# A two-layer decoder block on one core: the rotary key stored over 128 rows, the compressed query taken unnormalised from the accumulators, and the low part of the next key placed between mask and maximum

## The reference, cut to what matters

```python
def mla_mixer(h, w_dq, q_norm, w_uq, w_o, k_nope, k_rope, v, cos_rh, sin_rh):
    cq = rms_norm(h @ w_dq, q_norm)
    q = (cq @ w_uq).reshape(bsz, s_len, B_HEADS, QK_NOPE_DIM + QK_ROPE_DIM)
    q_nope = q[..., :QK_NOPE_DIM]                                  # 128 wide
    q_rope = apply_rope(q[..., QK_NOPE_DIM:], cos_rh, sin_rh)      # 64 wide
    ...
        logits = (einsum(qn, k_nope) + einsum(qr, k_rope)) * scale # 8 heads, k_rope shared by all
        logits = where(kpos <= qpos, logits, -inf)
        p = softmax(logits)
        return einsum(p, v)
```

## Time and profile before

| | |
|---|---|
| Median of three runs | 2006.02 us |
| Profiled execution, its own time | 2004.04 us |
| Its span, first to last instruction | 2001.7 us |
| PE busy | 1953.9 us (98%) |
| DVE, ACT, POOL busy | 967.7, 701.1 and 56.0 us |
| Mean granted TensorE clock | 0.991 of full |

### The profile page before, as it was taken

The page is one execution under the profiler, slowest core; times in us unless marked ns, Lnnn a source line. Parts: engine busy times, 40 slices in busy tenths (PEclk is TensorE's granted clock), DMA queues, the critical chain, the costliest instruction groups (busy, mean ns, idle before and its releaser), DMA issues.

```text
span 2001.7 us, 25843 instructions
## 1 busy us (share of the span) xinstructions
PE 1953.9 (98%) x9999; PEld 1662.5 (83%) x9999; DVE 967.7 (48%) x1399; ACT 701.1 (35%) x1095; POOL 56.0 (3%) x56
## 2 busy tenths in 40 slices
PE   7999999989999999999999999999899999999998
PEld 5888888978889888888998888889777898888888
DVE  5544432467655544442285444324766464444323
ACT  3332322345535323232253232223555442332222
POOL 0000000011100000000000000000000000000000
PEclk9999999999999999999999999999999999999999
DMA  5333333312213232333223333332211223333331
GB/s 159 102 88 105 87 95 109 88 43 84 74 54 95 84 105 84 105 87 108 80 76 104 105 90 99 95 97 83 58 38 53 64 64 105 100 89 102 98 95 43
DMA packets 344630, 174.64 MB, mean 87 GB/s; under 512 B 12159, under 2 KB 344045, under 8 KB 344557
## 3 DMA queue, kind: packets, MB, share of 16 engines
q1 hardware_dynamic: 341728, 171.47, 30.1%
q10 hardware_dynamic: 2828, 2.15, 0.4%
HBM read 171.50 MB, written 2.10 MB: 87 GB/s over the span
## 4 chain that ended last, share of the span: by engine, by line
PE 91%; DVE 5%; ACT 2%; issue 1%; DMA 1%; POOL 0%; SPq 0%; ACTq 0%; DVEq 0%
PE acc L1344 26%; PE acc L1346 26%; PE acc L1345 26%; PE sco L1344 3%; PE sco L1346 3%; PE sco L1345 3%; PE aux L1372 1%; DVE xT L941 1%; DVE y L934 1%; ACT prob_odd L656 1%; PE acc L1528 1%; DMA raw<-in_ffn_w_dram 1%; ACT tmp L644 1%; DVE mx L1061 1%; PE aux L1379 1%
## 5 line engine op out<-in xcount | busy, mean ns | idle before, releaser
L1344 PE MATMUL acc<-xg,wh 128*128 128x512 f32 (+1 forms) x1832 | 687.8, 375 | 15.4 <-DVE kh L1255 4.5
L1346 PE MATMUL acc<-xg,wl 128*128 128x512 f32 (+1 forms) x1832 | 680.5, 371 | 0.0
L1345 PE MATMUL acc<-xg,wh 128*128 128x512 f32 (+1 forms) x1832 | 680.3, 371 | 0.0
L876 DVE TENSOR_TENSOR wl<-raw,wh 128x1024 fp32r<-128x1024 f32 (+1 forms) x332 | 385.8, 1187 | 178.6 <-ACT wh L530 172.3
L1344 PEld LDWEIGHTS acc<-xg,wh 128*128 128x128 f32 x1832 | 346.3, 189 | 78.9 <-issue 4.4
L1345 PEld LDWEIGHTS acc<-xg,wh 128*128 128x128 f32 x1832 | 346.2, 189 | 60.0 <-issue 1.7
L1346 PEld LDWEIGHTS acc<-xg,wl 128*128 128x128 f32 x1832 | 346.1, 189 | 59.5
L530 ACT ACTIVATE wh<-raw 128x1024 fp32r<-128x1024 f32 (+1 forms) x332 | 327.0, 1023 | 141.6 <-PE acc L1346 86.0
L1346 PE MATMUL acc<-hT,wl 128*128 128x512 f32 (+1 forms) x704 | 255.2, 362 | 0.0
L1345 PE MATMUL acc<-hT,wh 128*128 128x512 f32 (+1 forms) x704 | 255.2, 362 | 0.0
L1344 PE MATMUL acc<-hT,wh 128*128 128x512 f32 (+1 forms) x704 | 255.2, 362 | 0.0
(11 more groups left out here) (221 smaller groups left out, 1847.5 us busy)
## 6 DMA issues: line engine op xcount, KB each, us to landing
raw<-in_ffn_w_dram SPq DMA_DIRECT2D x240, 512.0 KB, 4.3
raw<-in_ffn_w_dram SPq DMA_DIRECT2D x32, 384.0 KB, 3.5
raw<-in_moba_w_qkv_dram SPq DMA_DIRECT2D x24, 512.0 KB, 3.8
raw<-in_moba_w_o_dram SPq DMA_DIRECT2D x8, 512.0 KB, 3.8
raw<-in_mla_w_o_dram SPq DMA_DIRECT2D x8, 512.0 KB, 4.1
raw<-in_mla_w_dq_dram SPq DMA_DIRECT2D x4, 512.0 KB, 4.0
raw<-in_mla_w_uq_dram SPq DMA_DIRECT2D x8, 256.0 KB, 2.9
raw<-in_w_ukv_dram SPq DMA_DIRECT2D x16, 128.0 KB, 3.5
```

Of the source, the lines that this page charges most:

```text
L876: v.tensor_tensor(wl[:, slot, 0:tiles], raw[:, slot, 0:tiles], f32(wh[:, slot, 0:tiles]), ALU.subtract).then_inc(w_lo, 1)
L1344: t.matmul(dst, w_h, m_h, start=start, stop=False)
L1345: t.matmul(dst, w_h, m_l, start=False, stop=False)
L1346: return t.matmul(dst, w_l, m_h, start=False, stop=stop)
```

## The change: what it does

Three parts, all in the MLA stage:

- The rotary key `krT` is stored once for each half, with the other 64 rows zero (multiplied by a mask column `row_half`), so that the rotary products of `scores` run over all 128 rows. This is one more ACT copy and one more DVE operation at the entry.
- The compressed query is no longer normalised. ACT writes its high part `cqT` from each accumulator as soon as its unit is done, and squares it from there; DVE writes the low part from the accumulator. `spread(N_PRE4)`, the copy to `Rb`, the four multiplications and one POOL power go; the first normalisation enters through the variance (`xvar`) from which `qscale` is made. Here `split(4)`, `split(5)`, `split(6)` stand apart instead of in a row.
- `softmax_max` is cut in two, `softmax_mask` and `softmax_max`, and in MLA the low part of the next key stands between them.

The mask now lies on top of `ck`, so POOL writes it after the low parts of `ckT` and `krT`, and the buffers of values, outputs and odd probabilities get other places. In MoBA the two softmax functions are called one behind the other, in the order of before.

```diff
+        mask = at("mask", [P, P], F32, base[0])
...
+        neghalf = sb("neghalf", [P, TS + 2])
+        row_half = neghalf[:, TS:TS + 2]
...
+        xvar = rsums
...
-        krT = over("krT", [P, 2, S], F32R)
+        krT = over("krT", [P, 2, 2, S], F32R)
...
-        cq = at("cq", [P, KQ, S], F32, oT_at)
+        cqT = at("cqT", [P, 2, KQ, S], F32R, oT_at)
+
+        oM = (at("oM_hi", [P, HEADS, S], F32R, xg_base), at("oM_lo", [P, HEADS, S], F32R, oT_at + 4 * HEADS * S))
...
             if n == N_CQ:
-                return (cosR, sinR)[i % 2]
+                return (cosR, sinR, T[2])[i - 1]
...
         def values_of(n):
 
-            if n < HEADS:
-                return vh[:, n % 2, 0], vh[:, n % 2, 1]
-            return tuple(xg[:, a, KQ + n % 2].rearrange("p (t d) -> p t d", d=P) for a in range(2))
+            return vh[:, n % 2, 0], vh[:, n % 2, 1]
+
+        def o_of(n, a):
+
+            return oT[:, a, n] if n < HEADS else oM[a][:, n - HEADS]
+
+        def q_of(_):
+
+            return lambda k: (cqT[:, 0, k], cqT[:, 1, k])
...
             post_norm(N_F2)
-            causal_mask(3, U0[5])
-            rsqrt(EV0[N_PRE4])
+            pool.wait_ge(cq_lo, KK + 2)
+            causal_mask(3)
             rope_add(4 * HEADS + 8, T[3][:])
-            rsqrt(EV0[N_CQ])
...
             def square(n, i, src):
 
-                bufs = 1 if n in POST_FFN else 2 if n == N_CQ else 3
+                bufs = 1 if n in POST_FFN else 3
...
                 s.activation(ckT[:, 0, i], ck[:, i], COPY).then_inc(cq_hi, 1)
-            s.activation(krT[:, 0], ck[:, KK], COPY).then_inc(cq_hi, 1)
-            for w in (4, 5, 6):
-                split(u + w)
-            for m in range(KQ):
-                act.wait_ge(evacuated, r + m + 1)
-                if m == 0:
-                    act.wait_ge(unit_done, u + KQ)
-                s.activation(xg[:, 0, m], cq[:, m], COPY, scale=gains[:, G_Q + m:G_Q + m + 1]
+            for i in range(2):
+                s.activation(krT[:, i, 0], ck[:, KK], COPY, scale=row_half[:, i:i + 1]).then_inc(cq_hi, 1)
+
+            def cq_hi_of(m):
+                act.wait_ge(unit_done, u + m + 1)
+                s.activation(cqT[:, 0, m], acc[m][:], COPY, scale=gains[:, G_Q + m:G_Q + m + 1]
                              ).then_inc(cq_hi, 1)
+                square(N_CQ, m, acc[m][:])
+
+            split(u + 4)
+            cq_hi_of(0)
+            split(u + 5)
+            cq_hi_of(1)
+            cq_hi_of(2)
+            cq_hi_of(3)
+            split(u + 6)
...
             direct("k", 0, kh[:, 0])
             probT_zeros()
-            for m in range(KQ):
-                square(N_CQ, m, cq[:, m])
             v_split(HEADS)
...
-            def softmax_max(n):
+            def softmax_mask(n):
 
                 dve.wait_ge(score_psum, 3 * (n + 1))
                 if n % HEADS == 0:
...
+
+            def softmax_max(n):
+
                 for c in range(TS):
                     bank, o = BANK[c]
                     ins = v.tensor_reduce(mx[:, c:c + 1], sco[bank][:, o:o + (c + 1) * P], AX_X, ALU.max)
...
+            for i in range(2):
+                v.memset(row_half[i * ROPE:(i + 1) * ROPE, i:i + 1], 1.0)
+                v.memset(row_half[(1 - i) * ROPE:(2 - i) * ROPE, i:i + 1], 0.0)
...
             x_squares(N_PRE4)
-            norm_var(N_PRE4)
             for i in range(KK):
                 dve.wait_ge(cq_hi, i + 1)
                 v.tensor_tensor(ckT[:, 1, i], ck[:, i], f32(ckT[:, 0, i]), ALU.subtract).then_inc(cq_lo, 1)
-            dve.wait_ge(cq_hi, KK + 1)
-            v.tensor_tensor(krT[:, 1], ck[:, KK], f32(krT[:, 0]), ALU.subtract).then_inc(cq_lo, 1)
-            norm_diag(N_PRE4, 0, 1.0, T[3])
-            for w in (4, 5, 6):
-                split(u + w)
-            norm_factor(N_PRE4)
-            for m in range(KQ):
-                dve.wait_ge(unit_done, u + m + 1)
-                v.tensor_tensor(cq[:, m], acc[m][:], Rb[:], ALU.mult).then_inc(evacuated, 1)
-            dve.wait_ge(evacuated, r + KQ)
-            for m in range(KQ):
-                dve.wait_ge(cq_hi, KK + 1 + m + 1)
-                v.scalar_tensor_tensor(out=xg[:, 1, m], in0=cq[:, m], scalar=gains[:, G_Q + m:G_Q + m + 1],
-                                       in1=f32(xg[:, 0, m]), op0=ALU.mult, op1=ALU.subtract).then_inc(cq_lo, 1)
+            for i in range(2):
+                dve.wait_ge(cq_hi, KK + i + 1)
+                v.scalar_tensor_tensor(out=krT[:, i, 1], in0=ck[:, KK], scalar=row_half[:, i:i + 1],
+                                       in1=f32(krT[:, i, 0]), op0=ALU.mult, op1=ALU.subtract).then_inc(cq_lo, 1)
+
+            def cq_lo_of(m):
+                dve.wait_ge(cq_hi, KK + 2 + m + 1)
+                dve.wait_ge(sq_ready, SQ0[N_CQ] + m + 1)
+                v.scalar_tensor_tensor(out=cqT[:, 1, m], in0=acc[m][:], scalar=gains[:, G_Q + m:G_Q + m + 1],
+                                       in1=f32(cqT[:, 0, m]), op0=ALU.mult, op1=ALU.subtract
+                                       ).then_inc(evacuated, 1)
+
+            split(u + 4)
+            cq_lo_of(0)
+            dve.wait_ge(var_psum, EV0[N_PRE4] + 1)
+            v.tensor_scalar(xvar[:], aux[:, 0:TS], EPS, None, ALU.add).then_inc(r_ready, 1)
+            split(u + 5)
+            for m in range(1, KQ):
+                cq_lo_of(m)
+            split(u + 6)
...
             dve.wait_ge(var_psum, EV0[N_CQ] + 1)
-            v.tensor_scalar(var[:], norm_bank[0][:, 0:TS], EPS, None, ALU.add).then_inc(var_ready, 1)
-            dve.wait_ge(rtok_ready, EV0[N_CQ] + 1)
+            dve.wait_ge(r_ready, EV0[N_PRE4] + 1)
+            v.scalar_tensor_tensor(out=var[:], in0=xvar[:], scalar=EPS, in1=norm_bank[0][:, 0:TS],
+                                   op0=ALU.mult, op1=ALU.add).then_inc(var_ready, 1)
+            dve.wait_ge(rtok_ready, RT0[N_CQ] + 1)
             v.tensor_scalar(qscale[:], rtok[:], B_SCALE, None, ALU.mult).then_inc(r_ready, 1)
             dve.wait_ge(r_ready, EV0[N_CQ] + 1)
...
-                softmax_max(n)
+                softmax_mask(n)
                 if nxt:
                     direct("k", h + 1, kh)
+                softmax_max(n)
                 if turn:
                     rotated()
                 if nxt:
...
-                        if not first and (p, k) == (1, 6):
+                        if not first and (p, k) == (1, 6) and n_pre != N_PRE4:
                             spread(n_pre)
...
                     ins = product(dst, qh[:, 0, c * P:(c + 1) * P], qh[:, 1, c * P:(c + 1) * P],
-                                  kh[:, 0, 0:w], kh[:, 1, 0:w], True, rope_rows is None)
-                    if rope_rows is not None:
-                        rr = slice(rope_rows, rope_rows + ROPE)
-                        ins = product(dst, qrT[rr, 0, c * P:(c + 1) * P], qrT[rr, 1, c * P:(c + 1) * P],
-                                      krT[rr, 0, 0:w], krT[rr, 1, 0:w], False, True)
+                                  kh[:, 0, 0:w], kh[:, 1, 0:w], True, rope is None)
+                    if rope is not None:
+                        ins = product(dst, qrT[:, 0, c * P:(c + 1) * P], qrT[:, 1, c * P:(c + 1) * P],
+                                      krT[:, rope, 0, 0:w], krT[:, rope, 1, 0:w], False, True)
                     if c:
                         ins.then_inc(score_psum, 1)
```

More of the change, by code:

```diff
@@ L93, in yoco_kernel @@
     EV0 = [sum(2 if i in POST_FFN + POST_WO else 1 for i in range(n)) for n in range(15)]
-    SPREAD0 = [EV0[n] - (n > N_CQ) for n in range(14)]
+    RT0 = [EV0[n] - (n > N_PRE4) for n in range(14)]
+    SPREAD0 = [RT0[n] - (n > N_CQ) for n in range(14)]
     SQ_LAST0 = [2 * sum(LAST[:n]) for n in range(14)]
@@ L200, in yoco_kernel @@
         oT = over("oT", [P, 2, HEADS, S], F32R)
-        cq = at("cq", [P, KQ, S], F32, oT_at)
+        cqT = at("cqT", [P, 2, KQ, S], F32R, oT_at)
+        oM = (at("oM_hi", [P, HEADS, S], F32R, xg_base), at("oM_lo", [P, HEADS, S], F32R, oT_at + 4 * HEADS * S))
         assert spot[0] <= h_base + 4 * 2 * KF * S
-        prob_odd = [at(f"prob_odd{i}", [P, POFF[TS]], F32, o) for i, o in enumerate((ckT_at, vh_at))]
+        prob_odd = [at(f"prob_odd{i}", [P, POFF[TS]], F32, o)
+                    for i, o in enumerate((ckT_at, xg_base + 4 * KD * S))]
         BANK = [(0, 2 * P), (0, 0), (1, 0), (2, 0)]
@@ L487, in rope_add, with causal_mask @@
                 g.tensor_tensor(dst, T[0][:], T[2][:], ALU.add).then_inc(roped, 1)
-            def causal_mask(count, free_after):
-                pool.wait_ge(unit_done, free_after)
+            def causal_mask(count):
                 g.memset(mask[:], 0.0).then_inc(mask_ready, 1)
@@ L1500, in att_dst, with scores @@
                 return att_banks[st][rr][:]
-            def scores(n, rope_rows=None):
+            def scores(n, rope=None):
                 if n:
@@ L1558, in out_proj, with heads_out @@
                 last = heads + HEADS - 1
+                def heads_out(cols=slice(0, S)):
```

(17 more changed lines are left out.)

33 lines of the change are left out of this document (17 added, 16 removed).

## The result

The changed kernel takes 1995.23 us (median of 5 runs, 1994.26 to 1995.87), the kernel before, run beside it, 2004.49 us (5 runs). The two medians differ by 9.3 us. The ratio on record, 0.9945 with a 95% interval of 0.9934 to 0.9956, is not the quotient of the two medians (0.9954) and stands for 11 us, 9 to 13: the changed kernel is faster by about ten. The forecast was 1990, its range 1985 to 1998. The profiled execution took 1994.26 us against 2004.04 before.

The account below looks back on a forecast made before the run. PE bounds the kernel (91% of the last-ending chain), so time is won only where it waits or runs slow. -11.2 - 4.9 + 1.3 = -14.8 us gives 1989.2 or 1991.2 by base; forecast 1990, range 1985 to 1998.

Parts of the forecast that it names:

- rival C: MLA stage: clock falls in the new waits, on three heads and the entry, costing 6.2 us; 1995.4 us; chance 0.08.
- Part 1: MLA scores: rotary key over 128 rows saves 1.4 us per head, 11.2 us over 8 heads.
- The rule by which a stream on one set of rows would be the slow one: MLA scores: weight loads show on one set of rows, 6.4 us more instead of 11.2 less; 2006.8 us; chance 0.02.
- Part 2: MLA entry: query from the accumulators brings the first scores 4.9 us earlier, PE then waiting 1.35 us.
- Part 3: MLA loop: low key part ahead of the maximum wins 2.6 us, loses 3.9 on turning heads; net +1.3 us.
- The likeliest case: Whole kernel: all three parts as forecast, clock at full speed; 1990 us, own range 1985.5 to 1995; chance 0.77.
- the reading of one row: PE clock: after 2.73 us of idle the next window was granted 1.00; after 3.17 us it was 0.50.
- Rival D: MLA loop: clock stays at 1.2 GHz across many heads; half the loop, 60 us, would give 2020 us; chance 0.03.
- The +3.9 that bounded part 3: MLA loop: upper bound of part 3's loss, if the exponentials follow the maximum by its full 2.15 us.
- rival E: MLA loop: turning heads lose nothing, so part 3 gives -5.2; -21.3 us in all, 1983.7 us; chance 0.04.
- A: MLA scores: late starts come from changing tensors, not rows; only -4.9 + 1.3 remain, 2000.4 us; chance 0.06.

Follow-up runs that it names:

- e1: The kernel before with part 1 alone (rotary key padded to 128 rows); 1994.6 us.
- e5: The kernel before, 64-row rotary key kept, score products regrouped so the row count changes 2 times a head instead of 8; 1998.8 us.
- e4: The changed kernel with the low part of the next key ahead of the maximum on heads 0, 2, 4, 6 alone; 1987.5 us.
- e3: The changed kernel with part 3 undone, the low part of the next key behind the maximum on all heads; 1990.0 us.
- e9: The kernel of e2 with nine added matmuls of 128x512 in the waits behind heads 1, 3 and 5; 2007.6 us.
- e2: The kernel before with part 3 alone, the low part of the next key between mask and maximum; 2024.2 us.
- e10: The kernel before with parts 1 and 3, without part 2; 1999.0 us.
- e7: The changed kernel, but on heads 1, 3, 5 ACT makes the next key's high part before the four exchange copies; 1993.6 us.
- e6: The kernel of e2 with the grouped score products of e5, row count changing 2 times a head instead of 8; 2008.0 us.
- e11: The kernel of e4 with six more matmuls of 128x512 in the wait before the first scores; 1987.1 us.
- e12: The kernel of e4 with the mean of the compressed query's squares ahead of head 1's query product instead of behind it; 1985.7 us.

## Why the prediction was right, and what it missed

The time lies in the range of 1985 to 1998, but just outside the forecast's own 1985.5 to 1995, which had the clock at full speed: it is the room left for rival C that holds it.

- **Part 1, -11.2 us: right.** Scores took 3.96 us (4.0 forecast), the loop of e1 is 11.2 us shorter, and e5 shows that the price hangs on the changes. The rule by which a stream on one set of rows would be the slow one (the Trainium skill, "TensorE: Matmul & The Clock Gate", Part 3) did not show: the matmuls of head 1, all on 128 rows, have no late starts.
- **Part 2, -4.9: right.** Entry 25.0 instead of 29.8. PE's wait moved to the first scores, 1.55 us (1.35 forecast). Those started at 1436.10 or, less the 1.1 by which the stage began later, 1435.0 (1434.8 forecast).
- **Part 3, +1.3 from the waits: right in kind, a little large.** Turning heads wait 2.2 us (2.3 forecast), exponentials are 1.4 later (1.3); the even heads won 3.1 (e4 against e3) and not 2.6, and the net is 0.9 (e9 against before).
- **The clock: the step that failed.** The likeliest case left it at full speed in the new waits; rival C, at 0.08, had it fall on three heads and at the entry, 1995.4 us. It fell at the first scores and behind two of the three heads, 4.6 us in time (5.1 by the windows). In the loop -11.2 + 0.9 + 4.6 is -5.7, as measured. With 1.1 us ahead of the stage, which no part of the change explains, this is why 1995.2 came and not 1990; that C's 1995.4 is so near is partly luck, as it priced four stretches (6.2 us) and not the 1.1. The step that failed is the reading of one row, in which 2.73 us of idle were followed by 1.00: the same wait is followed by half clock in the profile of the changed kernel (0.62 from 420 to 424), and heads 1 and 3 differ in the same way.
- **Rival D was underrated in kind.** The changed kernel doesn't do it, but only because part 1 came with part 3: e2 is 19 us slower. The +3.9 that bounded part 3 above was no bound; e2's loop grew by 21.3, 17.1 of them by part 3.
- **A slip in rival E.** From the 2004.04 that A starts from, -21.3 gives 1982.7 and not 1983.7. Nothing hangs on it.

What stays open: why the wait behind head 3 passes without a fall (in e10 and e7 too), what starts the fourth stretch in e2, and whether the rows themselves or what they leave idle make the stretches long (e6).

## What to carry to other kernels

Price a change of the row count in a PE stream by the change (here 11.2 / 64 to 9.5 / 48, 0.18 to 0.2 us), so pad, or group the products by rows. When an edit gives PE one wait of a microsecond or two more, put a stretch at half clock into its price (it comes in one execution and not in the next, so one row at full clock is no evidence), and look at what PE runs right behind it: full-row matmuls got over it in some 3 us, a stream of half 64-row ones in 10 to 14 (e2). Before moving an operation ahead on one engine, check on each kind of iteration whether its input is there; where it isn't, leave it where it was (e4).

## What the hardware showed that I had not expected

- Useless matmuls can pay: 27 of 128x512 in waits made the kernel of e2 some 17 us faster (2024.2 to 2007.6) and the loop of the changed one 3.3 us shorter.
- Two parts interact through the clock: part 3 costs 17.1 us of loop without part 1 and 4.0 with it.
- A stretch at half clock needs no wait in front of it. In e4's output projection PE is busy throughout, and the granted clock falls in the window after narrow matmuls of the mean (1581.5 to 1583.6). The same matmuls pass at 1.00 in the changed kernel, e11 and e12:

```profile
1581.00:1584.00 3.00, 3.00 (x29) 3.00 (x28) 0.16 (x1) 0.34 (x1) 0.00 (x0) 1.00 0.02 5
1584.00:1587.00 3.00, 3.00 (x20) 2.91 (x19) 0.43 (x1) 0.85 (x1) 0.71 (x1) 0.67 0.00 0
1587.00:1590.00 3.00, 3.00 (x21) 2.91 (x20) 2.73 (x4) 1.02 (x4) 0.00 (x0) 0.76 0.04 13
```
